# First layer's first tile summed by TensorE, and two sums moved behind the first softmaxes

## The reference, cut to what matters

```
x = deepnorm(x, mix, ln_g[layer, 0], ln_b[layer, 0])     # layer_norm(alpha * x + mix)
ffn = grouped_moe(x, ...)                                 # y[token] = sum of 2: gate * expert(x[token])
x = deepnorm(x, ffn, ln_g[layer, 1], ln_b[layer, 1])
# layer 0: mix = conformer_conv(x); layer 1: mix = attention(x), keys and values from the same x
```

## Time and profile before

| what | value |
|---|---|
| median of 3 runs | 1076.39 us (1073.59 to 1077.23) |
| the profiled execution | 1078.42 us, its span 1076.8 us |
| PE busy | 939.6 us, 87% of the span |
| DVE busy | 450.1 us, 42% |
| ACT, POOL busy | 179.5 and 185.8 us, 17% each |
| mean granted clock of PE | 0.957 |

### The profile page before, as it was taken

One profiled execution on the slowest core, in us unless ns is written; L12 is line 12 of the kernel. 1 busy time (PEld: TensorE's weight loads), 2 busy tenths in 40 slices (PEclk: granted clock), 3 DMA queues, 4 the chain that ended last, 5 costly groups with the idle time before them and its releaser, 6 DMA issues.

```text
span 1076.8 us, 15571 instructions
## 1 busy us (share of the span) xinstructions
PE 939.6 (87%) x6018; PEld 501.8 (47%) x6018; DVE 450.1 (42%) x909; ACT 179.5 (17%) x394; POOL 185.8 (17%) x304
## 2 busy tenths in 40 slices
PE   6999989999997889795787999989979777998994
PEld 4444345566543444442443444546745343544541
DVE  3899973652111112110785547566512121111116
ACT  0000032421111000000223232435201000110000
POOL 1320020213211212001330001011230112122022
PEclk9999999999998999998898899988989899999998
DMA  9994389987999999999740004220899999999953
GB/s 291 379 410 158 83 306 399 376 359 280 379 391 376 419 362 403 383 428 393 257 180 1 0 1 156 79 79 40 352 325 380 382 403 400 378 414 351 412 186 117
DMA packets 74615, 308.70 MB, mean 287 GB/s; under 512 B 9423, under 2 KB 21627, under 8 KB 58010
## 3 DMA queue, kind: packets, MB, share of 16 engines
q1 hardware_dynamic: 36320, 229.53, 55.6%
q10 hardware_dynamic: 28218, 51.93, 13.1%
q0 software_dynamic: 9984, 25.97, 6.8%
HBM read 250.33 MB, written 53.74 MB: 282 GB/s over the span
## 4 chain that ended last, share of the span: by engine, by line
PE 43%; issue 19%; DMA 19%; DVE 16%; POOL 2%; ACT 1%; POOLq 0%; DVEq 0%; ACTq 0%; SPq 0%
PE ps L798 15%; DMA wring<-in_moe_w_up_dram 12%; DVE arena L1163 8%; PE ps L808 7%; PE ps L693 5%; PE ps L818 3%; PE ps L620 3%; DMA wring<-in_moe_w_gate_dram 3%; DMA arena<-xs_dram 2%; PE ps L828 1%; POOL rstd L1974 1%; PE ps L581 1%; PE ps L966 1%; DVE bns L1177 1%; PE ps L906 1%
## 5 line engine op out<-in xcount | busy, mean ns | idle before, releaser
L798 PE MATMUL ps<-wring,arena 128*64 128x256 f32 x1504 | 174.3, 386 | 22.7 <-DMA wring<-in_moe_w_gate_dram 12.8
L798 PEld LDWEIGHTS ps<-wring,arena 128*64 128x64 f32 x1504 | 108.1, 138 | 84.1 <-DMA wring<-in_moe_w_gate_dram 16.3
L620 PE MATMUL ps<-arena,wring 128*128 128x512 f32 x256 | 110.4, 593 | 1.5 <-DVE arena L1121 1.5
L1367 DVE COPY arena<-ps 128x256 f32<-128x256 f32 x32 | 13.6, 425 | 216.8 <-PE ps L906 206.0
L1163 DVE SCALAR_TENSOR_TENSOR arena<-arena,dwT 128x512 f32<-128x512 f32 x145 | 102.3, 780 | 0.0
L1988 POOL DMA_DIRECT2D arena<-xs_dram x112 | 59.5, 538 | 200.2 <-DVE arena L1346 159.9
L994 PE MATMUL ps<-wring,arena 128*128 128x512 f32 x192 | 87.9, 614 | 3.0 <-ACT arena L1821 3.0
L808 PE MATMUL ps<-wring,arena 128*64 128x512 f32 x384 | 86.5, 592 | 0.6 <-DVE arena L1367 0.6
L798 PE MATMUL ps<-arena 128*64 128x256 f32 x544 | 66.7, 401 | 17.6 <-DMA arena<-in_moe_w_gate_dram 9.7
L620 PEld LDWEIGHTS ps<-arena,wring 128*128 128x128 f32 x256 | 48.5, 190 | 62.0 <-issue 60.3
L1974 POOL TENSOR_TENSOR rstd<-vareps,half 128x1 f32<-128x1 f32 x20 | 23.7, 1186 | 283.5 <-DVE vareps L1180 283.5
(11 more groups left out here) (244 smaller groups left out, 1113.2 us busy)
## 6 DMA issues: line engine op xcount, KB each, us to landing
wring<-in_moe_w_up_dram SPq DMA_DIRECT2D x24, 2048.0 KB, 23.0
wring<-in_moe_w_down_dram SPq DMA_DIRECT2D x24, 2048.0 KB, 21.3
wring<-in_moe_w_gate_dram SPq DMA_DIRECT2D x23, 2048.0 KB, 22.8
xs_dram<-zero ACTq DMA_DIRECT2D x2, 16384.0 KB, 50.4
arena<-in_moe_w_gate_dram SPq DMA_DIRECT2D x9, 2048.0 KB, 26.6
arena<-in_moe_w_up_dram SPq DMA_DIRECT2D x8, 2048.0 KB, 26.2
arena<-in_moe_w_down_dram SPq DMA_DIRECT2D x6, 2048.0 KB, 23.3
xs_dram<-arena ACTq DMA_DIRECT2D x60, 128.0 KB, 8.7
```

The lines of the kernel that those rows point to most:

```text
L620: last = pe.matmul(ps[:, 2 * (c % 4) + h, :], w[:, k, h, (c % 2) * P:(c % 2) * P + P], xT[:, k, :], start=(k == 0), stop=(k == KD - 1))
L798: mm = pe.matmul(ps[h * CAP:(h + 1) * CAP, bank, 0:256], act[:, k, :], w[:, k, h * 256:(h + 1) * 256], start=(k == 0), stop=(k == KD - 1))
```

## The change

`SUMMED = (1, T)` says how many tiles of each layer are summed by PE: now one in the first layer, four in the second as before. The code of the second layer's sums is generalised and used for tile 0 of the first layer, with its small matrices in the unused quarters of `lnrow`. Experts 14 and 15 of the first layer are written back only after the gather of tile 0 has landed. Tiles 2 and 3 of the first layer are gathered into slot 5 of `wring` instead of LATE, and joined by DVE behind the first and the second softmax. The core of the diff:

```diff
-        yg_slots = [(6, 7), (7, 5)]
+        yg_slots = [(6, 5), (7, 5)]
...
+        SUMMED = (1, T)
...
+            sp.wait_ge(s_ln, 2 * T)
             weights(1, 0)
...
-            def sums():
-
-                pe.wait_ge(s_diag, 1)
-                pe.wait_ge(s_picked, 2)
-                pe.wait_ge(s_sg, DEPTH * E)
-                done = pe.snap(g, min_val=1, max_val=4096)
-                for t in range(T):
+            def sums(l):
+
+                pe.wait_ge(s_diag, l + 1)
+                pe.wait_ge(s_picked, 2 * (l + 1))
+                pe.wait_ge(s_sg, E * (l + 1))
+                for t in range(SUMMED[l]):
...
-                    if l == 1 and 8 <= e < 10:
-                        turn_picks(e - 8)
+                    if 8 <= e < 10:
+                        turn_picks(l, e - 8)
...
-            idle(0, 32)
+            sums(0)
+            idle(3, 32)
...
-                    if l == 1 and e < 8:
-                        pick(e - 2)
+                    if e < 8:
+                        pick(l, e - 2)
...
+                    if t < SUMMED[l]:
+                        dve.wait_ge(s_sum, t + 1)
+                        own(dve.tensor_tensor(x_sb[:, t, :], x_sb[:, t, :],
+                                              ps[:, 2 * t:2 * t + 2, :].rearrange("p a b -> p (a b)"), ALU.add))
+                        norm_x(t, n + t, l, 1)
+                        continue
...
-            combine(0, n, range(T - 1))
+            combine(0, n, range(2))
...
-                    combine(0, n - T, range(T - 1, T))
+                    combine(0, n - T, range(2, 3))
...
+                    if t == 0 and kh == 0:
+                        combine(0, n - T, range(3, T))
...
-                    if l == 1 and e in KEPT:
+                    if e in KEPT:
                         return
...
+                if l == 0:
+                    act.wait_ge(s_yg[0], 32)
+                    act.wait_ge(s_yc, E)
+                    for b, e in enumerate(KEPT):
+                        send(e, b)
...
-            for t in range(T - 1):
-                gated_y(0, t)
...
-                    pool.wait_ge(s_y[b], 32 * (8 * (l + 1) - l))
+                    pool.wait_ge(s_y[b], 32 * (8 * (l + 1) - l - (l == 0)))
+                pool.wait_ge(s_dn, E * (l + 1) - 1)
                 pool.wait_ge(s_oy, stored)
...
+                    if l == 0 and t == 1:
+                        inverse_std(n)
+                        for b in range(2):
+                            pool.wait_ge(s_y[b], 32 * 8)
```

More of the change, by code:

```diff
@@ L1100, in _ @@
             experts(1)
-            sums()
+            sums(1)
         @block.vector
@@ L1400, in experts, with pick @@
                     step(e, e // 2, e % 2, last=e == E - 1)
-                    if l == 1 and e < 8:
-                        pick(e - 2)
+                    if e < 8:
+                        pick(l, e - 2)
                 copy_h(E - 1, 1, True)
-            def pick(part):
+            def pick(l, part):
                 if part == 0:
-                    dve.wait_ge(s_kept, 1)
+                    dve.wait_ge(s_kept, l + 1)
                 elif part < 3:
-                    for t in range(2 * part - 2, 2 * part):
+                    tiles = range(2 * part - 2, min(2 * part, SUMMED[l]))
+                    for t in tiles:
@@ L1417, in pick @@
-                    own(dve.tensor_tensor(gate_far, gate_w[:, :, :], hit, ALU.subtract))
+                    seen = slice(0, SUMMED[l])
+                    own(dve.tensor_reduce(hit[:, :, seen], hits[l], AX.X, ALU.add))
+                    own(dve.tensor_tensor(gate_far[:, :, seen], gate_w[:, :, seen], hit[:, :, seen], ALU.subtract))
                 elif part == 4:
-                    both = [hits[:, j, :, :].rearrange("p t (i n) -> p (t i) n", i=2).unsqueeze(2).to_broadcast([P, 2 * T, 2, CAP])
-                            for j in range(2)]
@@ L1421, in pick @@
-                    dve.tensor_tensor(picks.rearrange("p t i d n -> p (t i) d n"), both[0], both[1], ALU.add
+                    both = [hits[l][:, j, :, :].rearrange("p t (i n) -> p (t i) n", i=2).unsqueeze(2)
+                            .to_broadcast([P, 2 * SUMMED[l], 2, CAP]) for j in range(2)]
+                    dve.tensor_tensor(picks[l].rearrange("p t i d n -> p (t i) d n"), both[0], both[1], ALU.add
                                       ).then_inc(s_picks, 1)
                 else:
-                    for t in range(T):
+                    for t in range(SUMMED[l]):
@@ L1786, in experts @@
                     store(e - 1, (e - 1) // 2, 1 - e % 2, e > 2)
[L1787 to L1789 removed]
+                    if 8 <= e < 10:
+                        act.wait_ge(s_picksT, 2 * l + e - 7)
+                        act.activation(picksT[l][:, e - 8, :], ps[:, 0, 0:P * SUMMED[l]], ACT.Copy).then_inc(s_picked, 1)
                     if l == 0 and e < 2 + T:
@@ L1855, in _ @@
                 if i == 1:
-                    gated_y(0, T - 1)
+                    for t in range(SUMMED[0], T):
+                        gated_y(0, t)
             act.dma_start(resrow, attn_bo[0].partition_broadcast(P)).then_inc(s_rows3, 16)
@@ L2032, in combine, with number_kept @@
                                                 ).then_inc(s_yg[t], 16)
-                    if t >= 2:
+                    if l == 1 and t >= 2:
                         inverse_std(n + t - 2)
-                for t in range(T - 2, T):
+                for t in range(T - 2 if l else 1, T):
                     inverse_std(n + t)
+            def number_kept():
+                pool.iota(rows_kept.rearrange("p (i n) -> p i n", i=2), pattern=[[S, 2], [1, CAP]], base=KEPT[0] * S,
+                          channel_multiplier=0, **exact).then_inc(s_kept, 1)
             for n in range(2 * T):
```

53 lines of the change are left out of this document (27 added, 26 removed).

## The result

The changed kernel takes 1082.99 us (median of 19 runs) where the kernel before takes 1076.35 (19 runs), 6.6 us more. The ratio on record, which is not that of the two medians, is 1.0085 with a 95% interval of 1.0063 to 1.0106; that is 9.1 us, between 6.8 and 11.4. So the loss is clear of the noise, and its size is 6.6 or 9.1 us. Forecast was 2.5 us; the median lies just inside the slow end of the stated range, 1083.2. The profiled execution has a span of 1084.3 us, 7.5 more than before, with a mean granted clock of 0.952 against 0.957.

The account below looks back on a forecast made before the run. PE was busy 87% of the span, so only its gaps at the two layer seams mattered. Head gain 5.5 less attention 4.0 leaves 1.5; tail loses 4.0: 2.5 us slower, 1078.9, range 1073.3 to 1083.2.

Parts of the forecast that it names:

- gain 5.5: Head, between the layers: tile 0's transposes start at 517.5 instead of 522.98, gain 5.5 us, between 4.7 and 7.5.
- First gather at 495.8, 0.5 after the product's end: Head: POOL issues tile 0's first gather 0.5 us after expert 14's down product, taken from 0 to 0.88.
- Landing in 8.0 as before: Head: tile 0's gathered rows land 8.0 us after the first gather, at 503.8, the queues being full as before.
- Clock costs 2.0 in the sum: Head: a clock fall during tile 0's sum costs 2.0 us, out of 0 to 2.75; sum at 511.3.
- DVE and the norm, 6.05 to tile 0's transposes: Head, after the sum: one DVE addition of 1.2 us and the norm of 4.85 precede tile 0's transposes.
- The transposes of the identity are 6.4 at half clock and end at 517.7, level with this; they cost nothing more.: Head, behind tile 0's sum: 6.4 us of identity transposes end level with tile 0's start at 517.5, extra cost 0.
- The attention gives back 4.0: Attention's first tile: DVE, with two joinings, becomes the bound; 4.0 of the 5.5 us gained are lost, 1.5 stay.
- The tail, loss 4.0: Second layer's end: POOL's new wait makes PE wait 2.6 us, plus 1.4 for a clock fall, 4.0 lost.
- Picks in the experts, 0: First layer's experts: added picks, transposes and copies cost 0 to 1 us, taken as 0.
- both gaps at half clock: Rival, head and tail: clock falls in both gaps, 5.9 us slower, 1082.3; half clock or a late tail 0.31.
- The first gather is held up: Rival, head: query-weight loads hold tile 0's rows until 511; 8 us slower, 1084.4; chance 0.05.

Follow-up runs that it names:

- e9: Changed kernel without the second layer's wait, identity transposes on both sides of tile 0's sum, one query-weight load held until tile 0's rows landed; ratio to before 1.0012.
- e2: Changed kernel with 48 more identity transposes ahead of tile 0's sum and 52 instead of 32 behind it; ratio to the kernel before 1.0028.
- e8: Changed kernel with 52 instead of 32 identity transposes behind tile 0's sum; ratio to the kernel before 1.0073.
- e13: Kernel before, unchanged, profiled once more; span 1069.7 us, 7.1 below its first profile. Its section also compares the table's thirteen profiles.
- e1: Changed kernel with POOL's new wait for expert 14's down product kept in the first layer only; ratio to the kernel before 1.0038.
- e4: Kernel before with only the second layer's gathers made to wait for expert 14's down product; ratio to the kernel before 1.0045.
- e10: Kernel before with the first layer's picks, diagonal and their two turns also made, read by nobody; ratio to the kernel before 1.0014.
- e3: Changed kernel with tile 2 joined ahead of the keys, only tile 3 behind the first softmax; ratio to the kernel before 1.0044.

## Why the prediction was wrong, step by step

The direction of the sum was right, its size was not: 2.5 us slower forecast, 6.6 measured by the medians and 9.1 by the ratio. The half that failed first is the head, **gain 5.5**. Its steps, against the first profile of before:

- *First gather at 495.8, 0.5 after the product's end.* It was 496.44. From ACT's copy released by the same product (495.49) POOL took 0.95; in the tail 0.94 (1037.70 to 1038.64). Of 0 to 0.88 the prediction took 0.5; the upper end was the right one, and a bit low.
- *Landing in 8.0 as before.* It was 9.4, and the head's range of 4.7 to 7.5 names no later landing. With the step before, the far part began 5.74 after the last product instead of 3.85, 1.9 late. What made the gather slower here is open (e9).
- *Clock costs 2.0 in the sum.* Measured 2.1 (511.58 - 505.83, less 3.64). Right here; with far parts of 5.54 to 6.54 against 3.67 in e2 it is 1.9 to 2.9 over the profiles without the first filling.
- *DVE and the norm, 6.05 to tile 0's transposes.* Measured 519.81 - 513.71 = 6.1. Right. Tile 0's transposes began at 519.81, forecast 517.5.
- *"The transposes of the identity are 6.4 at half clock and end at 517.7, level with this; they cost nothing more."* **This is the step that failed.** The clock had come back during the sum ahead of them, so they took 3.71, not 6.4; PE then idled for 2.60 and the clock fell a second time. The eight transposes took 1.56 instead of 1.16 and the products 23.38 instead of 20.84: 2.9 us. e8 and e2 remove the gap and the loss with it, and the thirteen profiles compared under e13 all agree. The prediction's own rows had it: with the clock back 5.5 us after work begins, so at 509.3, transposes that start at 511.3 run at full clock and end some 2.5 us before 517.5. No rival of the prediction had a second fall.

Of the 5.5 us, 2.2 were gone at tile 0's transposes, 1.9 of them by the late rows, and 2.9 went to the second fall, so 0.4 was left at tile 0's scores, against the first profile of before. Against the mean of the three profiles with the old head (47.5, 49.2, 48.0) the changed one is 1.1 us sooner, in part since e13 has the second fall as well.

- *The attention gives back 4.0.* From the start of the first joining to `turn(0, 1)` it is 572.37 - 550.43 = 21.9, forecast 22.3; from there to `turn(0, 3)` 19.8, forecast 19.5. In sum 41.7 against 37.7 before, 4.0 as forecast. POOL's additions moved onto the rotation of the queries, as said. The Trainium skill, GPSIMD Engine Reference, Specifications, has the two engines contend for SBUF where VectorE's operation has two inputs there; the trace agrees (2.57 and 2.45 for two such operations, where the next like one takes 0.42). With little gained in the head, all of the 4.0 became a loss.
- *The tail, loss 4.0.* Right mechanism, mis-sized by 1.0: 5.0 in the profile, some 5 and 4.8 timed (e1, e4). Of the wait of 3.28 (forecast 2.6) some 0.4 is POOL's later start; the clock cost 1.7 (forecast 1.4), though not in every profile.
- *Picks in the experts, 0.* Nothing shows against it (e10), in an interval from 0.2% faster to 0.5% slower.

From the scores' 0.4 sooner and the attention's 4.0, `turn(0, 3)` is 3.6 later; 1.3 of that is made good by the second layer's first expert, and with the tail's 5.0 that makes 7.3 us more than in the first profile of before (317.0 against 309.7). The timed loss is 6.6 or 9.1. The rival *both gaps at half clock* gave 1082.3, near the result, and half of its mechanism is there: the clock fell in both gaps. But it had the head still gain 4.75, so that its number is near is luck. *The first gather is held up* is not what happened: the rows came at 505.8, not 511.

**What stays open.** With all three causes repaired the time is, twice, 0.1% longer than before, each time within 0.3% of no change. The seams are 3 to 5 us shorter, but up to the experts, plus tail, the repaired kernel has 304.2 and 305.4 us where two executions of the kernel before have 309.7 and 304.1. So no run shows that the repaired kernel gains, and none shows either that the change costs something elsewhere: the scatter of one kernel is as large as the gain looked for. The picks alone show no cost (e10), and neither do the stretch ahead of the first seam and the second layer's experts. It wasn't tried whether the later first weight load of the second layer or the late writes of experts 14 and 15 cost anything.

## What to carry to other kernels

Matrix products that only keep TensorE busy have a length in time that follows its clock: count them for the full clock (here 0.11 to 0.12 us each, against 0.20 at half), and look at what stands ahead of them, since work that restores the clock halves them. A wait that is written for one use of a shared routine is paid in every use; here a line written for the first layer cost 5 us in the second, nearly as much as the head was to bring. And a saving ahead of a chain on another engine is worth only what that chain leaves: lay the moved work out on the engine that will be waited for next.

## What the runs showed of the hardware that was not expected

- A pair of indirect gathers of 128 rows of 4 KB each took 9.0 to 9.7 us from the first issue to the landing with weight loads in flight (ten profiles, up to ACT's late write), 6.2 to 7.0 at the second layer's end (1045.59 - 1038.64 in the changed kernel), and 8.0 in the kernel before behind ACT's write. With one of the loads held back it was 9.0.
- From the start of ACT's copy of a product to the indirect DMA that POOL issues on the same product pass 0.92 to 0.96 us (fifteen places, in the ten profiles with the change and in e4).
- Ahead of tile 0's transposes PE gaps of 2.37 to 2.60 us were followed by half clock in five profiles of five. In the tail gaps of 2.27 (e3), 3.03 and 3.28 were, gaps of 2.48 and 2.49 (e8, e2) were not: there the length of the gap alone doesn't tell, and the difference is 1.7 us.
- Two executions of the kernel before differ by 3.4 us in the sixteen experts of the second layer (267.2 and 263.8) and by 5.5 between the last expert product of the first layer and the first of the second (272.7 and 267.2).
